# Normalised x, two plain fp32 units and another division of work ahead of the attention of a hybrid trunk

## What is computed

```
xn   = rmsnorm(h, norm1_g)
proj = xn @ w_in            # 3*256 (q, k, v), 512 (u), 2*1024 (gates)
attn = stick_breaking(rmsnorm(q), rmsnorm(k), v)         # 4 heads of 64
y    = S5(u)                # 32 groups, state 64, complex diagonal, + D*u
ssm  = g * sigmoid(g @ w_glu + b_glu),  g = gelu(y)
h    = h + (sigmoid(gate_a) * (attn @ w_attn_proj) + sigmoid(gate_s) * (ssm @ w_ssm_proj)) @ w_o
h    = h + (silu(conv_g) * conv_v) @ w_down,  conv = causal_dwconv3(rmsnorm(h) @ w_up)
```

## Time and profile before

| what | value |
|---|---|
| median of 3 runs | 779.51 us (776.04 to 787.32) |
| profiled execution, its own time | 779.93 us |
| span of that execution (first to last instruction) | 778.2 us |
| TensorE busy | 729.7 us (94%) |
| VectorE, ScalarE, GpSimd busy | 445.8, 306.7, 154.6 us |
| mean granted TensorE clock | 0.971 |

### The profile page before, as it was taken

The page is one execution under the profiler, slowest core; times in us unless marked ns, Lnnn a source line. Parts: engine busy times, 40 slices in busy tenths (PEclk is TensorE's granted clock), DMA queues, the critical chain, the costliest instruction groups (busy, mean ns, idle before and its releaser), DMA issues.

```text
span 778.2 us, 13794 instructions
## 1 busy us (share of the span) xinstructions
PE 729.7 (94%) x5448; PEld 693.0 (89%) x5448; DVE 445.8 (57%) x634; ACT 306.7 (39%) x456; POOL 154.6 (20%) x184
## 2 busy tenths in 40 slices
PE   4995869899999998999999999999999999999997
PEld 2994759899899998999999999999999998888886
DVE  3795699754556766564467566566665665131211
ACT  5622213223367776543444343443433433122121
POOL 3079885360000000232211101101101101000000
PEclk9997977999799999999999999999999999999999
DMA  7332201324431021242323323223223233235331
GB/s 212 96 99 81 70 28 36 90 57 108 107 116 55 29 61 48 70 122 77 88 82 97 94 81 102 87 81 107 82 82 107 81 96 107 74 106 153 93 88 40
DMA packets 138886, 67.86 MB, mean 87 GB/s; under 512 B 23339, under 2 KB 137231, under 8 KB 138847
## 3 DMA queue, kind: packets, MB, share of 16 engines
q1 hardware_dynamic: 138687, 67.29, 30.9%
q10 hardware_dynamic: 160, 0.02, 0.0%
HBM read 61.85 MB, written 4.26 MB: 85 GB/s over the span
## 4 chain that ended last, share of the span: by engine, by line
PE 78%; DVE 9%; ACT 6%; POOL 4%; issue 2%; DMA 1%; ACTq 0%; POOLq 0%; DVEq 0%
PE ps L1585 70%; ACT hi L760 2%; PE ps L1711 1%; PE ps L1778 1%; PE ps L1706 1%; DVE lo L1087 1%; PE ps L1682 1%; DVE awl L1349 1%; ACT aw L894 1%; PE ps L1770 1%; ACT aw L889 1%; DMA stack<-in_ssm_d_dram 1%; ACT aw L898 1%; ACT xtok L787 1%; PE ps L1794 1%
## 5 line engine op out<-in xcount | busy, mean ns | idle before, releaser
L760 ACT ACTIVATE hi<-raw 128x1024 fp32r<-128x1024 f32 (+2 forms) x104 | 113.7, 1093 | 346.3 <-PE ps L1585 313.8
L1585 PE MATMUL ps<-xh,hi 128*128 128x258 f32 (+1 forms) x1120 | 233.4, 290 | 0.3 <-DVE lo L1087 0.3
L1585 PE MATMUL ps<-xh,lo 128*128 128x258 f32 (+1 forms) x1120 | 229.6, 287 | 0.0
L1585 PE MATMUL ps<-xl,hi 128*128 128x258 f32 (+1 forms) x1120 | 229.6, 287 | 0.0
L1087 DVE TENSOR_TENSOR lo<-raw,hi 128x1024 fp32r<-128x1024 f32 (+2 forms) x104 | 136.9, 1317 | 126.0 <-ACT hi L760 125.8
L1585 PEld LDWEIGHTS ps<-xh,hi 128*128 128x128 f32 x1120 | 178.1, 194 | 2.5 <-issue 1.1
L1585 PEld LDWEIGHTS ps<-xl,hi 128*128 128x128 f32 x1120 | 177.9, 193 | 0.0
L1585 PEld LDWEIGHTS ps<-xh,lo 128*128 128x128 f32 x1120 | 177.3, 193 | 0.0
L743 POOL TENSOR_TENSOR cv<-cv 128x512 f32<-128x512 f32 x22 | 28.4, 1290 | 230.2 <-DVE cv L1543 230.2
L1585 PE MATMUL ps<-ah,hi 128*128 128x512 f32 x176 | 69.8, 396 | 0.0
L1543 DVE SCALAR_TENSOR_TENSOR cv<-ut,cols,cv 128x512 f32<-128x512 f32 x88 | 65.9, 749 | 6.4 <-ACT cv L1037 0.9
(11 more groups left out here) (280 smaller groups left out, 972.9 us busy)
## 6 DMA issues: line engine op xcount, KB each, us to landing
raw<-in_w_up_dram SPq DMA_DIRECT2D x88, 256.0 KB, 3.1
raw<-in_w_in_dram SPq DMA_DIRECT2D x52, 256.0 KB, 3.3
raw<-in_w_down_dram SPq DMA_DIRECT2D x16, 384.0 KB, 3.3
raw<-in_w_down_dram SPq DMA_DIRECT2D x16, 320.0 KB, 4.0
raw<-in_w_o_dram SPq DMA_DIRECT2D x16, 256.0 KB, 3.1
xtok<-in_x_dram SPq DMA_DIRECT2D x4, 512.0 KB, 5.5
raw<-in_w_ssm_proj_dram SPq DMA_DIRECT2D x8, 256.0 KB, 2.8
out_dram<-yt SPq DMA_DIRECT2D x8, 256.0 KB, 2.2
```

Of the source, the lines that this page charges most:

```text
L760: act.activation(hi[slot][:, 0:n * P], raw[slot][:, 0:n * P], ACT.Copy)\
L1585: ins = pe.matmul(o, weights[w], acts(a, c), start=start and i == 0, stop=stop and i == 2)
```

## The change

Everything is ahead of unit 18 or in what it leaves behind.

- x is normalised in token layout: the squares of tokens 0 to 143, their mean, root and Newton step come first, then ScalarE and VectorE scale `xtok` in place, then it is transposed; the same for the other tokens. `hT` holds the normalised x. The spread row `rb` is now the root mean square itself (`rt[:, 3]`), and GpSimd multiplies `hT` by it later, to get h back for the residual (`h_raw`). Units are no longer multiplied by `rb`.
- Units 0 and 1 (`U_PLAIN`) are plain fp32 products of `raw`, which GpSimd scales by norm1_g (`plain_weights`), with `hT`. Their weights and the x split are off their path; the split of x runs beside them. SP loads units 2 and 3 when units 0 and 1 are done.
- `idle_products`: four products without use ahead of and behind the first transpose on TensorE.
- `small`, `powers`, `b_factor`, all turns (j = 0 to 6) and `decay` are on GpSimd, in one chain; three `hout` buffers; `out_map` puts output map 1 and half of 2 and 3 on VectorE.
- ScalarE empties the banks of units 0 to 17, of `spread`, of `kern`, and does the first scaling of a norm; VectorE empties gates 18 to 25 by a copy.
- Order of units: u, k, q, v, gates (in `GATE_ORDER`); new `STEPS` and `MOVES`. Norms and turns of v alternate between banks 4 and 6. Newton in three operations for four.

The core of the diff:

```diff
-STEPS = {0: [("spread", 0), ("columns", 0), ("small", 0)],
-         1: [("columns", 1), ("powers", 0)], 2: [("b_factor", 0)], 5: [("norm", 0), ("prep", 0)],
-         6: [("norm", 1), ("turn_v", 0)], 7: [("turn_v", 1), ("turns", 0), ("state", 0)],
-         8: [("prep", 1)], 9: [("norm", 2), ("readout", 0)],
-         10: [("norm", 3), ("state", 1)], 11: [("prep", 2)], 12: [("readout", 1)],
-         13: [("state", 2)], 14: [("prep", 3)], 15: [("readout", 2)],
-         16: [("state", 3)], 17: [("readout", 3)],
+STEPS = {2: [("columns", 0)], 3: [("spread", 0)], 4: [("columns", 1)],
+         5: [("norm", 0)], 6: [("norm", 1)], 7: [("prep", 0), ("out_map", 1)],
+         8: [("norm", 2), ("norm", 3)], 9: [("state", 0)], 10: [("prep", 1), ("out_map", 2)],
+         11: [("readout", 0), ("state", 1)], 12: [("prep", 2), ("out_map", 3)],
+         13: [("readout", 1), ("state", 2)], 14: [("prep", 3)],
+         15: [("readout", 2), ("state", 3)], 16: [("turn_v", 0), ("turn_v", 1)],
+         17: [("readout", 3)],
...
-         5: [("u_write", 3), ("u_read", 1)], 6: [("toep", 0)], 10: [("y_write", 0), ("toep", 1)],
-         11: [("u_read", 2)], 13: [("y_write", 1), ("toep", 2)], 14: [("u_read", 3)],
-         16: [("y_write", 2), ("toep", 3)], 19: [("y_write", 3)], 20: [("y_read", 0)]}
+         5: [("u_write", 3), ("u_read", 1)], 9: [("toep", 0)],
+         13: [("u_read", 2), ("toep", 1), ("y_write", 0)],
+         15: [("u_read", 3), ("toep", 2), ("y_write", 1)],
+         17: [("toep", 3), ("y_write", 2)], 19: [("y_write", 3)], 20: [("y_read", 0)]}
+NORM_BANK = (4, 6, 6, 4)
+TURN_BANK = (4, 6)
+HOUTS = 3
...
+            def plain_weights(unit):
+                pool.wait_ge(raw_in[unit], 32)
+                for k in range(KD):
+                    o = raw[unit][:, k * P:(k + 1) * P]
+                    ins = pool.tensor_scalar(o, o, g1[:, k:k + 1], None, ALU.mult)
+                ins.then_inc(w_scaled, 1)
...
+            pool.wait_ge(g1_set, 1)
+            plain_weights(0)
+            plain_weights(1)
+            small()
+            powers()
+            b_factor()
             input_map(0)
             pool.wait_ge(ct_set, 1)
             pool.wait_ge(xt_ps, 2 * KD)
-            pool.wait_ge(ss_set, NXT + 1)
-            output_map(0)
-            for j in range(5):
+            output_map(0, (0, 1))
+            turn_powers()
+            for j in range(7):
                 extend_turns(pool, link, j, pt)
+            link(pool.tensor_copy(decay[:, :, 1:NC], sm[:, S_D2, :].unsqueeze(2)
+                                  .broadcast_to([P, PAIRS, NC - 1])))
             pool.nop().then_inc(rot_set, 1)
-            pool.wait_ge(rot_set, 1)
             input_map(1)
-            output_map(1)
+            output_map(2, (1,))
+            input_map(2)
+            output_map(3, (1,))
+            input_map(3)
...
+                act.wait_ge(ss_ps, i + 1)
+                if i:
+                    act.wait_ge(normed, i)
+                act.activation(halves(tb[:, 0:2 * w], w), psum2(NORM_BANK[i], w), ACT.Identity,
+                               bias=eps[:], scale=1.0 / DH).then_inc(ss_v, 1)
...
+                act.wait_ge(k_ps, r + 1)
+                if r:
+                    act.wait_ge(kern_out[r - 1], 16 * T8)
+                for g in range(2):
+                    ins = act.activation(kern[:].rearrange("h (r g) c -> h g r c", g=2)[:, g],
+                                         ps[2 * GH * g:2 * GH * g + GH, 6, :]
+                                         .rearrange("h (r c) -> h r c", c=P), ACT.Copy)
+                ins.then_inc(kern_raw, 1)
...
+            def out_map(r):
+                if r == 1:
+                    dve.wait_ge(pw_set, 1)
+                    for u in u_out:
+                        dve.wait_ge(u, 16)
+                if r >= HOUTS:
+                    dve.wait_ge(y_ps, r - HOUTS + 1)
+                for c in (0, 1) if r == 1 else (0,):
+                    map_part(dve, link, r, c, mod[:].rearrange("p i r c -> p (i r c)"))
+                dve.nop().then_inc(h_dve, 1)
...
+            for unit in range(U_PLAIN):
+                pe.wait_ge(w_scaled, unit + 1)
+                for c in range(2):
+                    if unit == 0:
+                        pe.wait_ge(xt_a, (c + 1) * KD // 2)
+                        pe.wait_ge(xt_d, (c + 1) * KD // 2)
+                    for k in range(KD):
+                        ins = pe.matmul(ps[:, 2 * unit + c, 0:HL], raw[unit][:, k * P:(k + 1) * P],
+                                        hT[:, k, c * HL:(c + 1) * HL], start=k == 0,
+                                        stop=k == KD - 1)
+                ins.then_inc(unit_done, 1)
```

More of the change, by code:

```diff
@@ L178, in hybrid_trunk @@
         HOUT = 2 * RP * (T8 + 1) * GH
-        vT = [gates[:, i * L:(i + 1) * L] for i in range(2)]
+        v_at = hout_end - HOUTS * HOUT - 2 * L
+        vT = [gates[:, v_at + i * L:v_at + (i + 1) * L] for i in range(2)]
         gate = [gates[:, i * LL:(i + 1) * LL] for i in range(16)]
@@ L721, in _ @@
             pool.wait_ge(masks_set, 4)
-            for unit in range(U_PROJ):
-                for name, i in STEPS.get(unit, []):
-                    if name == "prep" and 1 <= i < ROUNDS - 1:
-                        input_map(i + 1)
-                        output_map(i + 1)
+            pool.wait_ge(rb_set, 1)
+            for k in range(KD):
+                pool.tensor_tensor(hT[:, k, :], hT[:, k, :], rb[:], ALU.mult).then_inc(h_raw, 1)
             for m in range(KD):
@@ L947, in gelu @@
                         .then_inc(gh_set, 1)
-            steps = {"norm": norm, "prep": prep, "readout": readout,
+            steps = {"norm": norm, "prep": prep, "readout": readout, "spread": spread,
                      "scores": scores,
@@ L1467, in _ @@
                 for name, i in STEPS.get(unit, []):
-                    if name in steps and name != "spread":
+                    if name in steps:
                         steps[name](i)
@@ L1604, in product, with idle_products @@
                 return ins
-            pe.wait_ge(masks_set, 1)
+            def idle_products(n):
+                for _ in range(n):
+                    pe.matmul(ps[:, 7, :], ones[:], bpair[:, 0].rearrange("p r c -> p (r c)")
+                              [:, 0:512], start=True, stop=True)
+            pe.wait_ge(masks_set, 2)
+            idle_products(2)
             pe.wait_ge(stack_full, 1)
@@ L1806, in run @@
                     pe.wait_ge(masks_set, 4)
-                if (name in ("norm", "turn_v", "prep", "state")
-                        or (name, i) == ("columns", 0)):
-                    for s_, n in used45:
+                bank = {"norm": NORM_BANK, "turn_v": TURN_BANK}.get(name, (0,) * 4)[i]
+                if bank == 4 or name in ("prep", "state", "scores") or (name, i) == ("columns", 0):
+                    for s_, n in used45 if name != "scores" else ():
                         pe.wait_ge(s_, n)
-                if name in ("spread", "prep", "readout", "scores") or (name, i) == ("columns", 1):
+                if bank == 6 or name in ("spread", "prep", "readout", "scores") \
+                        or (name, i) == ("columns", 1):
                     for s_, n in used67:
@@ L1858, in _ @@
                 else:
-                    ready = x_ready if unit == 0 else None
-                    width, col0 = (HL, 0) if unit < U_Q else (HLL, LATE0)
-                    ins = product(slot, 0, KD, bank, width, x_pair, col0, ready=ready, seen=KD)
+                    ready = x_ready if unit == U_PLAIN else None
+                    late = U_Q <= unit < U_V or unit >= U_GATE
+                    width, col0 = (HLL, LATE0) if late else (HL, 0)
+                    ins = product(slot, 0, KD, bank, width, x_pair, col0, ready=ready)
                 ins.then_inc(unit_done, 1)
```

504 lines of the change are left out of this document (267 added, 237 removed).

## The result

| | before | after |
|---|---|---|
| median of the runs, us | 781.68 (776.04 to 787.32, 4 runs) | 759.31 (758.32 to 760.03, 4 runs) |
| ratio, 95% interval | | 0.9707 (0.9644 to 0.977) |
| profiled execution, us; its span | 779.93; 778.2 | 760.03; 758.3 |
| first scores at, us | 217.9 | 195.9 |

The change makes the kernel 2.9% faster. By the profiled executions it wins 19.9 us (by the medians 22.4), where the prediction had 28.2. The part behind them took 2.1 us more, with the same waits; 2.0 of these lie in the down projection, whose blocks of output take 15.83 us each, where they took 15.56.

What follows compares the result with a forecast made beforehand. Bound: the stretch before the scores, 63 to 126 us above all, with VectorE and GpSimd full, TensorE waiting and half clock after stalls. Scores at 190 instead of 218.2 save 28.2 us: 779.93 becomes 751.7, called 751; range 739 to 767.

Steps and rivals of the forecast that it cites:

- the signs by which I was to be wrong: Input map 1 still running beyond 109 us, tap move ending after 138, or short holes between units bringing half clock back.
- Front: Everything until unit 2: unit 2 starts between 34.6 and 39.6 us, taken as 38.5 against 38.96 before; gain 0.5 us.
- the idle products may win a little: Front, on TensorE: the inserted idle products might bring unit 2 somewhat ahead of 38.5 us; no size given.
- prep(0): TensorE arrives at 79.2 us; the 5.3 us GpSimd wait and 3.2 us VectorE norm wait go; 8.6 us gained.
- GpSimd's chain: GpSimd's operations from 25.7 us up to input map 1, done at 102 to 104 us; a chain of 78 us.
- The stall of 5.0 us at state(0): Units 8 to 11: TensorE waits from 96.2 to 101.2 us behind VectorE's output map 1 and norms; bounds none to 8.
- prep(1) at 109.3: VectorE reads the banks at 109.3 us, just at TensorE's arrival; GpSimd ready at 104; prep(1) ends at 112.3.
- (a): Rival: VectorE and GpSimd pay contended prices throughout, GpSimd's chain ends at 120, prep(1) 11 us late; 767; 0.25 with (d).
- (d): Rival: SP's queue is late, lo(13) and lo(15) slips pass to readouts, 5 us twice; 761; 0.25 with (a).
- (c): Rival: GpSimd's chain becomes the bound, 112 us instead of 78, kernel slower than before; 780 to 795 us; chance 0.03.
- (b): Rival: holes close fully, unit 2 at 34.6, no stall, no clock loss; 740 us; chance 0.17.
- 756 us: Forecast if the skill's exclusion holds strictly: VectorE products take 2.1 us, ten cost 5 us more, the stall is 10.

Runs made afterwards that it cites:

- experiment 5: The idle products taken out, once of the changed kernel (761.71 us) and once of the kernel of experiment 2 (755.35 us).
- experiment 1: Against the changed kernel, GpSimd makes input map 1 ahead of the turns instead of behind them; 765.63 us.
- experiment 2: Against the changed kernel, small, powers and b_factor go back to VectorE and GpSimd begins with the turn powers; 753.49 us.
- experiment 4: Against the changed kernel, VectorE's lo splits of units 2 to 9 do only 16 of 1024 columns, dropping those weights' low part; 753.65 us.

## Why the prediction was right and wrong

Faster by more than 2%, as forecast; the median lies 8.3 us above the 751 named and inside its range. The path that gave 751 did not happen: it had one stall, at state(0), and no wait on GpSimd at prep(1), and the kernel has it the other way round. That the number still came near is in part luck, since a gain of 11.4 us that I had not counted stood against a chain that came 15 us late. Two of the signs by which I was to be wrong appeared: input map 1 ran until 118.0 us (I had set 109), and the tap move ended at 144.6 (138), that one only because all behind the hole was late. The clock in 63 to 126 us was 0.84, for "0.9 or more". By its steps:

**Front: mis-sized, 4.0 us too late.** Unit 2 started at 34.5, the lower bound, and I took 38.5. I had priced the transposes at 0.263 and added 2.05 us for products at 1.2 GHz; yet the earlier trace rows has the granted clock at 1.00 over those products, so the rows showed that they were slow and not that the clock was. With the idle products a transpose took 0.178 in the first 24, and unit 2 started 14.05 us behind the first plain product, in place of 14.2 + 2.05. The step that failed is "the idle products may win a little": experiment 5 puts them at 2.0 to 3.4 us at unit 2.

**prep(0): right in kind.** No wait on GpSimd, none on VectorE's norm; 74.2 for 79.2, of which 4.0 is the front.

**GpSimd's chain: the step that failed.** "Done at 59 ... 94 ... input map 1: 102 to 104", 78 us from its start, and it took 95.4, though it began 3.1 us before the 25.7 named. Term by term, forecast and measured: small and powers 11 and 15.1; b factor 6 and 6.6; input map 0 8 and 9.1; output map 0 8.5 and 9.1; turn powers 10 to 13 and 15.5; turns j = 0 to 4 13.5 and 21.1; j = 5 7.5 and 7.0; j = 6 2 and 2.0; decay 1.3 and 1.1; input map 1 8 and 8.1. The long operations were priced within 1.1 us each group. The excess is in the short ones, and in the turns j = 0 to 4 above all, where I went below the 15.75 us that the earlier trace rows showed without giving a reason. 13.5 is about their price alone: by the undisturbed ones in the trace after, 0.30, 0.33, 0.39, 0.49 and 0.70 us from start to start for j = 0 to 4, the thirty come to 13.2 us. But VectorE was busy 13.7 of the 21.1 us beside them, where it had been busy 6.9 of the 15.75 before. Output map 1, which the change puts on VectorE, ran beside the first six turns and cost them 3.0 us; two norms and two splits ran beside the others.

**The stall of 5.0 us at state(0): it wasn't there, for a reason of the same kind.** I gave VectorE 1.6 us a product of output map 1 by the earlier trace rows. It paid 0.76, because GpSimd was at 16-column operations at that moment, and those paid. With long ones beside it the 1.5 us came, and a stall: 2.6 us in experiment 1, 3.0 in experiment 2.

**prep(1) at 109.3, with GpSimd "5 us early": wrong.** TensorE was there at 97.9, 11.4 us earlier than forecast (4.0 front, 5.0 no stall, 2.4 the rest), and GpSimd at 118.0, 15 later than 103. The 6 us of slack became a hole of 20. All that TensorE had won ran into it, and this is where the expected gain went: prep(1) 8.9 us late, and 2.4 over the 3.0 that I had given it, by half clock, so unit 12 started at 134.3, 11.2 us after the forecast 123.1. Behind it 5.3 came back, and the first scores, forecast at 190, started at 195.9: no more half clock (2.5), 5.8 us from readout(3) to the scores for 7.3, and small things.

**Rivals.** The mechanism that happened is (a)'s, with GpSimd at 118 for 120; I gave it and (d) together 0.25. Its 767 us was 8 too high: prep(1) came 1.8 us earlier than it had, the half clock cost 2.4 there in place of 5, and 5.3 us came back behind unit 12; the 2.1 us more behind the scores went the other way. (c) was far off: it asked for 112 us of chain. (d) didn't occur: neither a readout nor a state waits for SP; the u reads took 3.75 us for 5.13. (b)'s 740 us wasn't reached by any version; the nearest are at 745 to 746.

**The Trainium skill** (SBUF — State Buffer, Who interferes with whom) states the exclusion, and the trace after agrees with its kind: 1.24 us for GpSimd's 32 columns on a 1.23 us split. For long operations the exclusion was not for their whole length: in experiment 2 a VectorE product and a GpSimd one passed together every 1.53 us (80.56 to 82.08 and 79.99 to 81.51), where their prices alone, 0.76 and 1.05, add up to 1.81. Taken as I did, as a price of VectorE's alone, it named the wrong payer; that its 756 us lies nearer the result than 751 is luck, since it came from a stall of 10 us at state(0), and there was none.

## What to carry to other kernels

When a chain moves from VectorE to GpSimd, price its short operations by what VectorE does at the time, not by their width: here one took up to as long as the VectorE product it met, where that had both inputs in SBUF. Add up both engines' work of this kind over the stretch almost as if it were one queue (three quarters of it came back in experiment 4), and look for a third place in time (here VectorE's idle 47 to 56 us) before looking for another order. And slack against a neighbour's arrival is worth only what that arrival is worth: the better the rest of the forecast does, the sooner the slack is gone.

## What I had not expected of the hardware

- Beside each other, a VectorE product with two SBUF inputs and a GpSimd operation slow above all the shorter: GpSimd's 16 columns 0.80 for 0.22 us while VectorE kept 0.76 on 576 columns; VectorE's 264 columns 1.43 for 0.43 us beside GpSimd's 576-column products (104.54 in experiment 2; the same product took 0.43 at 112.88 in the kernel before). Where both are long, both pay: VectorE 1.49 for 0.76, GpSimd 1.45 for 1.05 (512 columns).
- With one input from PSUM a VectorE product of 264 columns took 0.41 to 0.43 us in every trace, also while GpSimd was at a 512-column product (109.93 after the change), and GpSimd's kept 1.10.
- Four products without use (eight records) ahead of the x transposes brought these from 0.260 to 0.178 us each in the first group, while the page's granted clock reads 1.00 in both kernels over that stretch. What makes the difference stays open.
- A wait of 2.6 us at 107 us was followed by 10 us at 1.2 GHz, while one of 1.2 us at about the same place in the kernel with norm 2 ahead of prep(0) was followed by none. The length of the wait doesn't decide it alone: with map 1 ahead of the turns a wait of 2.6 us at 91.2 us was followed by none either, the 32 products of state(0) taking 1.20 us as at the full clock (1.21 in the kernel after), and the granted clock read 1.00 there.

```profile
93.83 1.20 PE L1793 MATMUL ps<-uc,win 128*64 128x66 f32 x32 [2.61 <-ACT gates L953]
```
